# A hybrid attention and SSD block on one Trainium2 core: all four heads' products of an SSD group in one slot, and the turns of units one slot sooner

## What is computed

```python
h = rms_norm(x, norm_mix_g)
q, k, v, z, xbc, dt_raw = split(h @ w_in)           # 2048 each, z 2048, xbc 4096, dt 64
attn = dilated_window_attention(...)                 # 16 heads of 128, three dilations
ssd  = ssd_mixer(z, xbc, dt_raw, ...)                # 8 groups of 4 heads of 64, chunks of 128, two directions
x = x + concat(attn, ssd) @ w_out
x = x + square(relu(rms_norm(x, norm_mlp_g) @ w_up)) @ w_down
```

```python
Lmat = exp(segsum(dt * A))                                       # decays of a head
y_diag = einsum('bclgn,bcsgn->bgcls', C, B) * Lmat @ (x * dt)    # of each direction
y = (y_fwd + y_bwd + xs * d_skip) * silu(z)                      # then a norm over each group's 256 columns
```

## Time and profile before

| | |
|---|---|
| median of 3 runs | 1536.33 us (1535.97 to 1536.65) |
| the profiled execution | 1537.11 us |
| its span, first to last instruction | 1535.4 us |
| TensorE (PE) busy | 1519.7 us, 99% |
| VectorE (DVE) busy | 944.6 us, 62% |
| ScalarE (ACT) busy | 773.1 us, 50% |
| DMA | 191 GB/s over the span |

### The profile page before, as it was taken

How to read it: one execution, slowest core, us unless ns; L and a number is a source line. 1 busy time by engine, 2 the same in 40 slices (tenths; PEclk the granted TensorE clock), 3 DMA queues, 4 the chain that set the end, 5 groups by cost and what they waited for, 6 DMA issues and landing times.

```text
span 1535.4 us, 20663 instructions
## 1 busy us (share of the span) xinstructions
PE 1519.7 (99%) x7166; PEld 1255.5 (82%) x7166; DVE 944.6 (62%) x1248; ACT 773.1 (50%) x1099; POOL 24.8 (2%) x36
## 2 busy tenths in 40 slices
PE   7999999999999999999999999999999999999998
PEld 5878888888888888888888888888888888888887
DVE  6788888888766666655554545454545445544542
ACT  6387777786644454544444444334433344333531
POOL 0000000000000000000000000000000000000000
PEclk9999999999999999999999999999999999999999
DMA  9676666665665666565556665666566656666564
GB/s 267 219 222 193 191 191 181 190 191 165 182 182 170 181 179 181 178 229 187 188 186 188 182 191 189 194 186 189 188 192 193 189 181 190 192 192 185 182 192 136
DMA packets 188213, 290.98 MB, mean 190 GB/s; under 512 B 13646, under 2 KB 69328, under 8 KB 188161
## 3 DMA queue, kind: packets, MB, share of 16 engines
q1 hardware_dynamic: 185440, 286.85, 62.2%
q10 hardware_dynamic: 2720, 3.45, 0.7%
HBM read 288.05 MB, written 5.34 MB: 191 GB/s over the span
## 4 chain that ended last, share of the span: by engine, by line
PE 96%; DVE 2%; ACT 0%; DMA 0%; issue 0%; SPq 0%; DVEq 0%; POOL 0%; ACTq 0%
PE psum L1211 93%; PE psum L1472 1%; DVE w_lo L797 1%; PE psum L1233 1%; PE psum L1312 0%; PE psum L1332 0%; PE psum L1249 0%; DMA x_in<-in_x 0%; DVE conv L837 0%; PE psum L1259 0%; ACT w_hi L489 0%; DVE dt_p L1041 0%; SPq L307 0%; DVE dt_r L1059 0%; DVE conv L833 0%
## 5 line engine op out<-in xcount | busy, mean ns | idle before, releaser
L797 DVE TENSOR_TENSOR w_lo<-raw,w_hi 128x1024 fp32r<-128x1024 f32 x512 | 608.6, 1220 | 134.7 <-ACT w_hi L489 131.1
L489 ACT ACTIVATE w_hi<-raw 128x1024 fp32r<-128x1024 f32 x512 | 522.9, 1054 | 294.0 <-DMA raw<-in_w_down 144.6
L1211 PE MATMUL psum<-w_hi,actT_lo 128*128 128x512 f32 x1280 | 508.1, 397 | 0.0
L1211 PE MATMUL psum<-w_lo,actT_hi 128*128 128x512 f32 x1280 | 500.1, 391 | 0.0
L1211 PE MATMUL psum<-w_hi,actT_hi 128*128 128x512 f32 x1280 | 499.9, 391 | 0.0
L1211 PEld LDWEIGHTS psum<-w_hi,actT_hi 128*128 128x128 f32 x1280 | 240.9, 188 | 51.5
L1211 PEld LDWEIGHTS psum<-w_hi,actT_lo 128*128 128x128 f32 x1280 | 241.0, 188 | 50.9 <-issue 3.6
L1211 PEld LDWEIGHTS psum<-w_lo,actT_hi 128*128 128x128 f32 x1280 | 241.1, 188 | 46.8
L1211 PE MATMUL psum<-w_hi,hid_lo 128*128 128x512 f32 x512 | 199.5, 390 | 0.0
L1211 PE MATMUL psum<-w_hi,hid_hi 128*128 128x512 f32 x512 | 199.2, 389 | 0.0
L1211 PE MATMUL psum<-w_lo,hid_hi 128*128 128x512 f32 x512 | 199.2, 389 | 0.0
(11 more groups left out here) (196 smaller groups left out, 990.9 us busy)
## 6 DMA issues: line engine op xcount, KB each, us to landing
raw<-in_w_in SPq DMA_DIRECT2D x128, 512.0 KB
raw<-in_w_up SPq DMA_DIRECT2D x128, 512.0 KB
raw<-in_w_down SPq DMA_DIRECT2D x128, 512.0 KB
raw<-in_w_out SPq DMA_DIRECT2D x64, 512.0 KB
raw<-in_w_in SPq DMA_DIRECT2D x64, 256.0 KB
raw<-in_w_in SPq DMA_DIRECT2D x128, 128.0 KB
decay<-decay_rows SPq DMA_DIRECT2D x16, 512.0 KB, 5.3
rel_tiles<-rel_rows ACTq DMA_DIRECT2D x1, 3072.0 KB, 23.2
```

The costliest lines, as they stand in the source:

```text
L489: act.activation(w_hi[j][:, :, :], raw[j][:, :, :], ACT.Copy).then_inc(hi_ready, 1)
L797: tt_(w_lo[j][:, :, :], raw[j][:, :, :], w_hi[j][:, :, :].bitcast(f32), ALU.subtract).then_inc(lo_dve, 1)
L1211: return pe.matmul(o, lhsT, rhs, start=first, stop=last, **kw)
```

## The change

Three edits. In TensorE's script the products of heads 0 and 1 (k = 5) and of heads 2 and 3 (k = 7) both go to k = 6, one batch behind the other, each with its waits. In ScalarE's script the decays of the next group's heads, which stood in k = 6, 7, 8 and 12, stand in k = 7, 8, 10 and 12. In TensorE's script the turns of units go from slots 1, 9 and 17 to slots 0, 8 and 16. The slots of `stage_unit` stay.

```diff
-DECAY_SLOTS = {6: 0, 7: 1, 8: 2, 12: 3}
+DECAY_SLOTS = {7: 0, 8: 1, 10: 2, 12: 3}
...
-                    if k in (5, 7):
+                    for h0 in (0, 2) if k == 6 else ():
                         pe.wait_ge(xtok_ready, G + 1)
-                        pe.wait_ge(mix_ready, 4 * G + k - 3)
+                        pe.wait_ge(mix_ready, 4 * G + h0 + 2)
...
-                            for h in (k - 5, k - 4):
+                            for h in (h0, h0 + 1):
...
-                if s in (9, 17):
-                    turn_unit(0, s // CH - 1)
...
+                if s in (8, 16):
+                    turn_unit(0, s // CH - 1)
...
-                    if s == 1:
+                    if s == 0:
                         turn_unit(m, 2)
-                    if s in (9, 17):
+                    if s in (8, 16):
                         turn_unit(w, s // CH - 1)
```

## The result

| | before | changed |
|---|---|---|
| median | 1536.49 us (4 runs, 1535.97 to 1537.85) | 1550.72 us (4 runs, 1549.62 to 1551.22) |
| ratio | | 1.0091, 95% interval 1.0078 to 1.0103 |
| profiled execution, its span | 1537.11, 1535.4 us | 1550.94, 1549.2 us |
| granted clock, mean of the span | 1.000 | 0.996 |

The change costs 14.2 us. The forecast was +7.6 us, 1543.9 us, with a range up to 1547.8: the sign was right, the size was not, and the range did not hold it. T is again the start of window 2, here 178.91.

The account below looks back on a forecast made before the run. PE, busy 99% of the span, was taken as the bound. Joining -3.0, slot 8 +9.1, slot 16 +0.6, first window +0.6 and slot 0 +0.3 gave +7.6 on 1536.33: 1543.9 us, range 1540.8 to 1547.8.

Parts of the forecast that it names:

- Joined products: Between chunks on PE, the second batch follows the first and the fixed 0.37 us is paid once: 8 groups, -3.0 us.
- the two readings weighed there: For the products batches: the fixed part belongs to the change of tile form (-3.0 us) or to each batch (0).
- Decays: In slot 8's window, ScalarE's decays of the next group's head 0 start at T + 10.8.
- Slot 16: PE's turn in slot 16 waits 0.2 us for ScalarE's copy, three times: +0.6 us.
- Rival (a): Not slower: the copy is done when PE comes to slot 8's turn, only joining counts; 1533.8 us, chance 0.07.
- rival (b): Stalls cost PE speed too: a slow chunk behind each of four long stalls, 9.4 us more, 1553.3 us; chance 0.07.
- matmuls after a stall 0.4 us apart: Sign in PE's changed profile that the forecast is wrong: matmuls come 0.4 us apart after a stall.
- the stalls of slot 8: PE's turn in slot 8 waits for ScalarE's copy in three windows: 3.2 + 3.2 + 2.7 = +9.1 us.
- the upper bound: For each stall in slot 8: 3.7 us, if VectorE's gate or the tanh is as late as before.
- window 0 and slot 0 of window 1: Early turns there: +0.6 us net after slot 20 swallows delay, and +0.3 us waiting for the copy in slot 0.
- first window: Slot 8's turn 2.4 us late, 1.9 swallowed by slot 20's wait: net +0.6 us, bounds 0.5 and 2.9.
- its lower end: Low end of the range: stalls of 2.5 us in slot 8, none in slot 16 and slot 0; about +4.5 us.

Follow-up runs that it names:

- join_only: The changed kernel with the turns of units back in slots 1, 9 and 17, leaving joined products and moved decays; 1533.75 us, ratio 0.998.
- old_decays: The changed kernel with the decays back in k = 6, 7, 8 and 12; 1572.71 us, ratio 1.023.
- tanh_first: The changed kernel with ScalarE's copy first in slots 8 and 16 and, in k = 10, the tanh ahead of head 2's decays; 1549.61 us.

## Why the prediction was wrong in size

**Right.** *Joined products* at -3.0: 2.97 us for each of eight batches, shown by join_only. (Of the two readings weighed there, the measurement fits the one by which the fixed part belongs to the change of form. The Trainium skill, TensorEngine Tiling (Array Packing), Key Properties, says that a change of tiling mode drains TensorE; that the 0.37 us are such a drain, no run here shows.) *Decays* at T + 10.8, and the moment at which PE could turn, T + 28.9, to 0.1 us. *Slot 16* at 3 x 0.2: 0.19, 0.19 and 0.23. The place and the cause of the stalls, PE's wait for `stage` in slot 8, and that slot 0 of windows 2 and 3 has none. Rival (a) asked for a copy done 3.2 us sooner; no run of the unchanged ScalarE order came near it.

**Failed, first: the step against rival (b), and with it its chance of 0.07 and its place outside the range.** It was argued from one place of one execution: 1.85 us of idle, and PE at its pace after it. The same wait in join_only's profile cost 1.65 us more. Counted from the moment at which PE could have gone on, 18 of PE's waits between 45 and 420 us in the twelve profiles took 2.0 to 2.3 us; 7 were followed by slow matmuls and 11 were not. The stalls at issue were longer, 2.7 to 3.7 us, and all three were followed by them, as were the eight of 3.3 to 4.6 us in old_decays and tanh_first. The Trainium skill's rule (the page and section above), which I had set aside for that one row, gave the right side here. The mechanism was in the text, and so was the test ("matmuls after a stall 0.4 us apart"). Its price was too high, since a whole slow chunk of 2.35 us was put behind each of four stalls, window 0's included: measured were 1.6 to 2.7 us behind three, 5.95 in all, and none in window 0 of the changed kernel's profile. With it the forecast would have been 7.6 + 5.95 = 13.6, 1549.9 us. With an argument of one row against it, and the profile's own first chunk for it, a chance near one half was due, and the range had to reach 1553.

**Mis-sized: the stalls of slot 8**, 3.2 + 3.2 + 2.7 forecast, 3.66 + 3.67 + 2.72 measured, +0.95. Windows 2 and 3 had the gate at T + 18.2, as late as before (18.0), the case that I had named for the upper bound; that a conversion which comes sooner would bring the gate sooner was the step that failed. VectorE's short wait (0.3 us) did go, but VectorE began its unbroken work 9.3 us before the window in place of 9.8 (165.01 against 174.84 in the kernel before), and that took it back. The 2.7 of the first of the three was right, and for the reason given: the squares of window 1 began at 113.95, right behind the conversion, without a wait. (The prediction's own terms give 2.8 or 2.9 for it, so the last 0.1 is luck. Its first window, 2.4 - 1.9, is 0.5 and not 0.6, and its lower end, with that term in it, +5.0 and not +4.5.)

**Mis-sized: window 0 and slot 0 of window 1**, +0.9 forecast, +0.4 measured. Slot 8's delay was 2.4 us as forecast (PE turns at 51.90; the place costs 3.75 us, where the spread and the turn cost 0.46 and 0.91 before). Slot 20 took up 2.1 of it (3.42 less 1.32), more than the idle 1.85 that I had set against it, and 0.3 was left. In slot 0 of window 1 the copy was ready within 0.1 us. Another 0.2 us less came from the start-up, which differs between the profiles of all these kernels (by 2 us) and is not the change's doing as far as they show.

## What to carry to other kernels

When PE is the bound and a change makes it wait, the wait's length is the lower end of the price: look up its stretch's granted clock in the changed trace, and put the fall of the clock into the forecast's range with a real chance, since one idle stretch that went without it in one execution is no evidence of much. Before an instruction is moved sooner, work out when its producer's engine gets to the work it waits for: here a copy at the end of ScalarE's slot made a slot's lead on PE worthless. Test by filling the wait with idle work: if the kernel gets faster though the wait's end stands, the loss was in the clock and not in the order.

## What the runs showed of the hardware

- Behind idle stretches of PE of 2.7 to 3.7 us the granted clock was at half (0.50 over 294 to 297 in window 3), 1.6 to 2.7 us lost each time in the changed kernel. Behind those of 2.0 to 2.3 us the fall came in some executions and not in others, for the same place: behind the wait in slot 8 of window 0, 2.19 us in eight kernels, the place cost 3.75 us in five and 5.35 in three. This may be a source of spread between executions, which was only argued: join_only's three runs at a mean clock of 1.000 took 1533.1 to 1533.8 us, its eight at 0.998 and 0.999 took 1532.6 to 1535.4. Another is the start-up: the twelve profiles come to the end of slot 8's chunk in window 0 between 47.5 and 49.5 us. From the start of window 5 to the end all twelve take the same 1128.65 us, to 0.02.
- Two batches of products on 64-column tiles, one behind the other, cost 2.97 us and not 3.34: the way in and out of that form, 0.37 us, is paid once.
- Slow matmuls in the records also lengthen PE's busy time (+3.6 us here), so 5.95 of the lost microseconds are counted as work: PE read 98% busy while 14 us were lost.
